# The logits of a decoder step's sample queries against cached keys: full float products replaced by three products of high and low parts

## The reference, cut to what matters

```python
def attend_selected(q, k_sel, v_sel, valid):
    bsz, t, h, d = q.shape
    qg = q.reshape(bsz, t, N_KV_HEADS, h // N_KV_HEADS, d)
    s = jnp.einsum('btgrd,btkgd->btgrk', qg, k_sel).astype(jnp.float32) * (d ** -0.5)
    s = jnp.where(valid[:, :, None, None, :], s, -jnp.inf)
    p = jax.nn.softmax(s, axis=-1).astype(v_sel.dtype)
    o = jnp.einsum('btgrk,btkgd->btgrd', p, v_sel)
    return o.reshape(bsz, t, h * d)
```

## Time and profile before

| what | value |
|---|---|
| median of 3 runs | 2142.6 us (2141.64 to 2146.61) |
| the profiled execution's own time | 2139.28 us |
| its span | 2137.2 us |
| mean granted clock of PE | 0.957 of full |
| PE busy | 1960.7 us, 92% of the span |
| DVE, ACT, POOL busy | 999.8, 684.2, 603.3 us |

### The profile page before, as it was taken

One profiled execution on the slowest core, in us unless ns is written; L12 is line 12 of the kernel. 1 busy time (PEld: TensorE's weight loads), 2 busy tenths in 40 slices (PEclk: granted clock), 3 DMA queues, 4 the chain that ended last, 5 costly groups with the idle time before them and its releaser, 6 DMA issues. The chain is left out here.

```text
span 2137.2 us, 30706 instructions
## 1 busy us (share of the span) xinstructions
PE 1960.7 (92%) x11034; PEld 1701.7 (80%) x11034; DVE 999.8 (47%) x1841; ACT 684.2 (32%) x929; POOL 603.3 (28%) x329
## 2 busy tenths in 40 slices
PE   7999999999999999998788789899688898999998
PEld 7999999998878887798674378899655565699897
DVE  4123333111143431422758956779979972321533
ACT  4243333112343332322446222222154452320410
POOL 4333333463334446455010011112110010035220
PEclk9999999999999999999898899999899999989999
DMA  6222222223322333210320212112220005341121
GB/s 183 71 68 79 79 78 69 62 86 89 89 78 79 88 89 88 90 40 20 135 50 2 48 56 82 30 30 92 96 84 0 1 1 178 104 163 41 39 62 42
DMA packets 240514, 152.85 MB, mean 72 GB/s; under 512 B 24946, under 2 KB 235634, under 8 KB 240050
## 3 DMA queue, kind: packets, MB, share of 16 engines
q1 hardware_dynamic: 228162, 136.27, 21.8%
q10 hardware_dynamic: 10192, 9.46, 1.3%
q0 software_dynamic: 2080, 6.09, 0.9%
HBM read 135.33 MB, written 16.43 MB: 71 GB/s over the span
## 5 line engine op out<-in xcount | busy, mean ns | idle before, releaser
L398 POOL TENSOR_TENSOR wlo<-wraw,whi 128x1024 fp32r<-128x1024 f32 x177 | 430.2, 2431 | 853.3 <-ACT whi L393 851.1
L410 PE MATMUL PS<-hhi_g,whi 128*128 128x288 f32 (+1 forms) x1152 | 324.1, 335 | 12.1 <-POOL wlo L398 7.2
L410 PE MATMUL PS<-hhi_g,wlo 128*128 128x288 f32 (+1 forms) x1152 | 317.2, 330 | 0.0
L410 PE MATMUL PS<-hlo_g,whi 128*128 128x288 f32 (+1 forms) x1152 | 316.8, 329 | 0.0
L410 PE MATMUL PS<-hhi,whi 128*128 128x364 f32 x1176 | 273.2, 341 | 28.5 <-DVE hlo L497 12.5
L393 ACT ACTIVATE whi<-wraw 128x1024 fp32r<-128x1024 f32 x177 | 186.7, 1055 | 343.3 <-PE PS L410 308.4
L410 PE MATMUL PS<-hlo,whi 128*128 128x364 f32 x1176 | 265.2, 334 | 0.0
L410 PE MATMUL PS<-hhi,wlo 128*128 128x364 f32 x1176 | 264.5, 334 | 0.0
L410 PEld LDWEIGHTS PS<-hhi,whi 128*128 128x128 f32 x1176 | 207.2, 194 | 36.0 <-issue 26.8
L410 PEld LDWEIGHTS PS<-hhi_g,whi 128*128 128x128 f32 x1152 | 195.8, 190 | 31.0 <-issue 6.6
L410 PEld LDWEIGHTS PS<-hhi_g,wlo 128*128 128x128 f32 x1152 | 196.3, 189 | 17.8
(11 more groups left out here) (333 smaller groups left out, 2689.9 us busy)
## 6 DMA issues: line engine op xcount, KB each, us to landing
wraw<-in_w_in_a_dram SPq DMA_DIRECT2D x96, 512.0 KB, 3.9
wraw<-in_w_out_a_dram SPq DMA_DIRECT2D x32, 512.0 KB, 4.0
wraw<-in_w_in_b_dram SPq DMA_DIRECT2D x25, 512.0 KB, 3.8
wraw<-in_w_pe_gate_dram SPq DMA_DIRECT2D x16, 512.0 KB, 4.1
kpg<-in_cache_k_dram SPq DMA_DIRECT2D x64, 128.0 KB, 2.1
vpg<-in_cache_v_dram SPq DMA_DIRECT2D x64, 128.0 KB, 2.1
xs<-xT SPq DMA_DIRECT2D x1, 4368.0 KB, 12.6
xT<-xs SPq DMA_DIRECT2D x1, 4368.0 KB, 14.1
```

Of the source, the lines that this page charges most:

```text
L398: nc.gpsimd.tensor_tensor(wlo[par][:], wraw[par][:], whi[par][:].bitcast(F32), ALU.subtract).then_inc(w_lo, 1)
L410: mm = nc.tensor.matmul(o, w[par][:, k, :], r(k, c0, cn), start=first and i == 0 and n == 0, stop=last and i == KD - 1 and n == 2)
```

## The change

The keys leave PSUM in two parts. ACT still copies each key head, now into `khiT` of type fp32r, and signals each head by a new semaphore `sa["kh"]`. DVE then subtracts this from PSUM to get `kloT` (`keys_lo`, one instruction of 128x1024 for each key head) and gives the signal `sa["ke"]` that ACT gave before. The queries are split once in `sample_operands` into `qbhi` and `qblo`. For each half and key head PE does three fp32r products in place of one full float product. The part of the new keys keeps full floats, but multiplies both parts of the queries. Two of the buffers of `gate_z` move elsewhere, since `kloT` takes their place.

```diff
--- before.py
+++ after.py
@@ -226,6 +226,8 @@
         qT = pl("qT", [P, NH, TP])
         sc = pl("sc", [P, block_off(NBLK)])
         scs = pl("scs", [NS, SLS])
+        KL0 = H1 + sum((w * 4 + 31) // 32 * 32 for w in (NH * TP, block_off(NBLK), SLS))
+        kloT = nc.alloc_sbuf_tensor_at("kloT", [P, NKV, PAST], F32R, offset=KL0)
         swp = pl("swp", [P, TP])
         tq = pl("tq", [P, TP])
         sqt = pl("sqt", [P, TP])
@@ -251,11 +253,14 @@
         iqb = pl("iqb", [P, DEC_B, NS])
         ikout = pl("ikout", [P, 9, ID])
         pl = region(X0, X0 + KD * TP * 4)
+        K2 = X0 + sum((w * 4 + 31) // 32 * 32 for w in (NKV * TP, 9 * NKV * DH))
         kT = pl("kT", [P, NKV, TP])
         vtok = pl("vtok", [P, 9, NKV * DH])
         csQ, snQ = pl("csQ", [P, TP]), pl("snQ", [P, TP])
         qb = pl("qb", [P, DEC_B, NKV, NS])
-        K2 = X0 + sum((w * 4 + 31) // 32 * 32 for w in (NKV * TP, 9 * NKV * DH))
+        qbhi = pl("qbhi", [P, DEC_B, NKV, NS], F32R)
+        qblo = nc.alloc_sbuf_tensor_at("qblo", [P, DEC_B, NKV, NS], F32R,
+                                       offset=K2 + 2 * ((TP * 4 + 31) // 32 * 32))
         kout = nc.alloc_sbuf_tensor_at("kout", [P, 9, NKV * DH], F32, offset=H1 + (IH // 2) * TP * 4)
         pl = region(D0, H1)
         PTs = pl("PTs", [P, NBLK, REP, P])
@@ -267,7 +272,9 @@
         vpg = [[t[:, 0:NPAGE // 2], t[:, NPAGE // 2:]] for t in vpg]
         vpg.append([nc.alloc_sbuf_tensor_at(f"vpg2{q}", [P, NPAGE // 2, NKV * DH], F32, offset=W0 + q * 2 * KD * P * 4)[:]
                     for q in range(2)])
+        KT0 = H2 + 2 * NPAGE * NKV * DH * 4
         kTb = pl("kTb", [P, NKV, PAST])
+        khiT = nc.alloc_sbuf_tensor_at("khiT", [P, NKV, PAST], F32R, offset=KT0)
         Ps = pl("Ps", [NS, SLS])
         PsT = pl("PsT", [P, 9, NS])
         amx, anb, asm, ars = (pl(n, [P, NBLK * NH]) for n in ("amx", "anb", "asm", "ars"))
@@ -283,7 +290,7 @@
         ROW = (TP * 4 + 31) // 32 * 32
         zb = [nc.alloc_sbuf_tensor_at(f"zb{f}", [P, TP], F32,
                                       offset=(D0 if f < 3 else H1 + NH * TP * 4) + f % 3 * ROW)
-              for f in range(6)] + [swp, tq]
+              for f in range(6)] + [sqt, rbc]
         ptab = fixed_ptab
 
         PS = ctx.enter_context(nc.psum_tensor("PS", [P, 8, BANK], F32))
@@ -353,7 +360,7 @@
         z_ev, z_in = sem("z_ev"), [sem(f"z_in{f}") for f in range(KD)]
         z_st = [sem("z_st0"), sem("z_st1")]
         at_ = {n: sem(f"at_{n}") for n in ("s", "mx", "nb", "ex", "rs", "dg", "tr", "pt", "pv", "o")}
-        sa = {n: sem(f"sa_{n}") for n in ("pre", "qc", "kt", "ke", "s", "mx", "nb", "ex", "nr", "tr", "pt", "pv", "o")}
+        sa = {n: sem(f"sa_{n}") for n in ("pre", "qc", "kt", "kh", "ke", "s", "mx", "nb", "ex", "nr", "tr", "pt", "pv", "o")}
         kpin, vpin = ([sem(f"{n}{q}") for q in range(3)] for n in ("kpin", "vpin"))
         oy = {n: sem(f"oy_{n}") for n in ("y", "hi", "lo", "xup")}
         xs = nc.dram_tensor("xs", [P, KD * TP], F32).ap()
@@ -1109,8 +1116,8 @@
                 if b:
                     act.wait_ge(sa["s"], b)
                 for g in range(NKV):
-                    last = nc.scalar.activation(kTb[:, g, :], PSF[:, (4 + 2 * g) * BANK:(6 + 2 * g) * BANK], ACT.Copy)
-                last.then_inc(sa["ke"], 1)
+                    nc.scalar.activation(khiT[:, g, :], PSF[:, (4 + 2 * g) * BANK:(6 + 2 * g) * BANK],
+                                         ACT.Copy).then_inc(sa["kh"], 1)
 
             kT_evac(0)
             for b in range(DEC_B):
@@ -1584,6 +1591,8 @@
                 idb = ident[0:NS, 0:NS].rearrange("p (b t) -> p b t", t=DEC_T)
                 nc.vector.reduce_sum(bd8[:], idb, axis=AX.X)
                 own.link(nc.vector.reduce_sum(d8[:], idb.rearrange("p b t -> p t b"), axis=AX.X))
+                own.link(nc.vector.tensor_copy(qbhi[:], qb[:]))
+                own.link(nc.vector.tensor_tensor(qblo[:], qb[:], qbhi[:].bitcast(F32), ALU.subtract))
                 nc.vector.tensor_tensor(qa8[:], d8[:].unsqueeze(1).broadcast_to((NS, NH, DEC_T)),
                                         qs[0:NS, 0, :].unsqueeze(2).broadcast_to((NS, NH, DEC_T)), ALU.mult).then_inc(sa["pre"], 1)
 
@@ -1626,11 +1635,26 @@
                 nc.vector.tensor_copy(qT[:, :, b * DEC_T:(b + 1) * DEC_T],
                                       PS[:, 3, 0:NS].rearrange("p (h t) -> p h t", t=DEC_T)).then_inc(sa["o"], 1)
 
+            def keys_lo(b, g):
+                dve.wait_ge(sa["kh"], 2 * b + g + 1)
+                if b and g == 0:
+                    dve.wait_ge(sa["s"], b)
+                last = nc.vector.tensor_tensor(kloT[:, g, :], PSF[:, (4 + 2 * g) * BANK:(6 + 2 * g) * BANK],
+                                               khiT[:, g, :].bitcast(F32), ALU.subtract)
+                if g:
+                    last.then_inc(sa["ke"], 1)
+
+            for g in range(NKV):
+                keys_lo(0, g)
             sample_max(0)
             for b in range(DEC_B):
+                if b + 1 < DEC_B:
+                    keys_lo(b + 1, 0)
                 dve.wait_ge(sa["ex"], b + 1)
                 own.link(nc.vector.reciprocal(srs[:, b:b + 1], ssm[:, b:b + 1]))
                 nc.vector.tensor_scalar(Ps[:], Ps[:], srs[:, b:b + 1], None, ALU.mult).then_inc(sa["nr"], 1)
+                if b + 1 < DEC_B:
+                    keys_lo(b + 1, 1)
                 if b:
                     sample_out(b - 1)
                 for f in range(2 * b - 4, 2 * b - 2) if 2 <= b < 6 else ():
@@ -2141,8 +2165,14 @@
                     pe.wait_ge(sa["ex"], b)
                 for m, (a, n) in enumerate(PARTS):
                     for g in range(NKV):
-                        nc.tensor.matmul(PS[0:NS, m, 0:n], qb[:, b, g, :],
-                                         kTb[:, g, a:a + n] if m < 2 else kT[:, g, 0:NS], start=g == 0, stop=False)
+                        if m == 2:
+                            for q in (qbhi, qblo):
+                                nc.tensor.matmul(PS[0:NS, m, 0:n], q[:, b, g, :].bitcast(F32), kT[:, g, 0:NS],
+                                                 start=g == 0 and q is qbhi, stop=False)
+                        else:
+                            for q, k in ((qbhi, khiT), (qbhi, kloT), (qblo, khiT)):
+                                nc.tensor.matmul(PS[0:NS, m, 0:n], q[:, b, g, :], k[:, g, a:a + n],
+                                                 start=g == 0 and k is khiT and q is qbhi, stop=False)
                     mm = nc.tensor.matmul(PS[0:NS, m, 0:n], repb[:, b, :], scs[:].bitcast(BF16)[:, a:a + n],
                                           start=False, stop=True)
                 mm.then_inc(sa["s"], 1)
```

## The result

The changed kernel takes 2159.37 us (median of 6 runs, 2155.86 to 2160.65) against 2143.09 for the kernel before. The ratio is 1.0071, with an interval of 1.0058 to 1.0084: slower by 15 us by the ratio, by 16 us between the medians. The profiled execution took 2160.08 us.

What follows compares the result with a forecast made beforehand. PE, with its clock, was taken to bound the sample turns before, the chain through DVE's subtractions after. Terms 5.95 + 3.7 + 1.1 + 2.05 = 12.8 us on 2142.6 gave 2155.4 us, range 2146 to 2165.

Steps and rivals of the forecast that it cites:

- The loop takes over from PE: Sample turns: PE waits about 1.5 us for DVE's subtractions; a full-clock turn lasts 12.72 us, where it lasted 11.7.
- The products: Logits of each turn: twelve fp32r products replace eight records, the new keys' part doubles; net gain 0.54 us a turn.
- Turns 1 to 6: Sample turns: 1.85 us less from their lengths, 7.8 us more for the clock; together +5.95 us.
- Turn 0: First sample turn: the loop adds 2.2 us, a clock falling with PE's longer wait 1.5 us; together +3.7 us.
- Start: First key copies to first logits: subtractions delay the logits 1.65 us, less 0.54 in the logits; +1.1 us.
- Split: Step 8 of the prompt's attention: query copy 0.75 us, subtraction 1.22, two gaps 0.08; +2.05 us, bounds 1.5 to 2.5.
- Why the clock falls: Sample turns: PE's idle 1.5 us just ahead of the logits makes the clock fall in every turn; 1.3 us a turn.
- (1): Sample turns: the clock never falls, so the change costs only +3.5 us, 2146.1 us; chance 0.14.
- (2): Sample turns: the clock stays low longer, 2.8 us in each of seven turns; 2165.7 us; chance 0.12.
- (3, 4): Subtraction runs in half the time, 2145.7 us, chance 0.05; products run faster, by the skill page's figure, 2145.6 us, chance 0.02.

Runs made afterwards that it cites:

- the products alone: Changed kernel without the subtractions of the keys, whose low part is left out; the three products and the query split stay: 2143.17 us, ratio 0.9995.
- the two orders of DVE that took the loss back: Changed kernel with both key subtractions behind reciprocal and scaling: 2155.11 us; the same with DVE's signal given for each key head: 2150.66 us.
- the kernel with the wide products: Changed kernel with five idle products of 448 columns between the two heads of each request's value products: 2157.22 us, ratio 1.0068.

## Why the prediction was right

The forecast was slower, 2155.4 us in a range of 2146 to 2165; it came out at 2159.4, and by the cause that was named for most of it, the loop through DVE's subtractions. What it put down for the clock came near enough to stay in the range, but not for the reason that it gave; so far it was luck. Its steps, with the profiled executions:

- **The loop takes over from PE.** Right, shown by the products alone (ratio 0.9995), by the subtraction done twice (+14.0 us), by the two orders of DVE that took the loss back, and by the wait for `kloT` in six of seven turns. The subtraction takes 1.217 us on average, 1.22 in the sum. The loop lasts 7.17 us, not 7.5: from the end of the first subtraction over the reciprocal and the scaling to the end of the second it is 2.0 us, and I had put 2.27. So PE waits 1.1 us, not 1.5.
- **The products** gain 0.41 us a turn, not 0.54. They do follow each other by 0.23 us at full clock, as in the earlier trace rows. The 131 ns of the Trainium skill ("TensorE: Matmul & The Clock Gate", section "Back-to-back issue gap") are not seen in this kernel.
- **Turns 1 to 6:** +7.9 for +5.95. At full clock they are 6 x 12.5 = 75.0 us (76.3 in the sum; the 12.5 is from the kernel with the wide products), so the clock took 86.1 - 75.0 = 11.1 us, 1.85 a turn, where I took 1.3. This is the term that was mis-sized. The clock took 8.2 us before and 10.4 us with the products alone, so most of its growth is there without the subtractions and their wait, as far as one profile of each can say. The loop itself, at full clock, added 75.0 - 70.0 = 5.0 us.
- **Turn 0:** +4.1 for +3.7. **Start:** +2.6 for +1.1. Here the clock fell within the first logits (0.73 from 1779.0 to 1785.4), which I had not allowed for. **Split:** +2.4 in its stretch for +2.05, with the wait at step 8 at 3.25 us for the 3.3 given.
- **Why the clock falls:** wrong. I put it on the idle time ahead of the logits. Filling that time changed turns 1 to 6 by 0.9 us in all; wide products within the values brought four of six turns, which had been at 0.76 to 0.88, to 1.00. The rule of the Trainium skill that I weighed ("TensorE: Matmul & The Clock Gate", section "HAM oscillation — how this bites in real kernels": waits between bursts put the engine back to half clock) fits turn 0, where PE waited 5.31 us and came back at half clock. It does not cover turn 1, nor the turns of the kernel before, where PE was busy all the time. The prediction took the five of them that paid without a wait as agreeing with the rule; they speak against it as the cause.
- **The rivals.** The clock did not hold (1); it took 1.85 us a turn and not 2.8 (2); subtraction and products run at the speed of their rows (3, 4).

The five columns of the table come to 17.4 us in the profiles, where the sum said 12.8. Most of the difference is in turns 1 to 6 and in the start, and there in the clock. The medians moved 16 us. How much each contributes to the median can't be told from one profile a kernel: turns of the changed kernel differ by 1.5 us, and the stretch ahead of step 8, the same in all kernels, by up to 7 us.

## What to carry to other kernels

Before work is taken from the engine that is busy all the time, walk the loop that its next task hangs on and count how much later that comes free: here 0.4 us of products was bought with 2.4 us of subtractions on a loop that had 1.2 us to spare. Where such work must be there, put it behind what others wait for, and signal it in the pieces in which it is needed. The order on DVE and a signal for each head, with the split in DVE's idle time, took back the whole loss within what can be measured (1.0071 to 1.0007). Read the granted clock of each turn beside its length, since a delay can cost more than itself.

## What the runs showed of the hardware that was not expected

- The clock of TensorE falls while the engine is busy without a gap, in products that move only 32 columns (PE busy 3.10 of 3.10 us at a clock of 0.55, turn 1 above). With five products of 448 columns between the two heads six turns in a row ran at 1.00 in one kernel, and four of six in another. Behind the last maximum of the first kernel the clock fell in spite of them, and one full float product in the same place of the kernel before gave three turns of six at 1.00 and a time 0.64% longer.
- At half clock the filling meant to help costs double: 2.13 us for five products that take 1.06 us at full clock.
- A cast of 128x1024 within SBUF to fp32r takes 0.69 us on DVE; a subtraction of the same size takes 1.22 to 1.23 us, from PSUM or from SBUF. At the end of the prompt's attention the subtraction from SBUF took 1.94 us, in each of the four kernels that have it there. POOL was multiplying (`rdiag`, 1.40 us) during a part of it; that this is the cause was not tested.
